# A trunk step on one core: reordering the normalization of the first token tile at the sub-layer boundaries

## The chip, the core and the metric

The kernel runs on one core of one Trainium2 chip. The metric is device time in microseconds (us) of one execution. Five engines run side by side, each through its own instruction list in order: TensorE (PE, matmuls), VectorE (DVE), ScalarE (ACT), GpSimd (POOL) and SyncE (SP, which starts the transfers here). They meet through semaphores only.

## What is computed

The reference is one step of a four-layer trunk over 128 context tokens and 256 sample tokens, model width 1024, all in fp32. Each layer has a half-step feed-forward (FFN), a mixer (attention, gated convolution or HGRN2) and a second FFN: twelve sub-layers. Cut to what matters here, every sub-layer is

```python
h = rmsnorm(x, g_pre) * (1 + scale) + shift        # modulated input of the sub-layer
o = sub_layer(h)                                   # ffn: (silu(h @ a) * (h @ b)) @ w_out
x = x + gate * rmsnorm(o, g_post)                  # and for an ffn half of it
```

So the input of each sub-layer needs the full output of the one before: two norms stand between the last product of one and the first product of the next.

## The kernel before, in words

**Tiles and products.** The 384 tokens are three tiles of 128 (t = 0, 1, 2). A product in full precision is made of three matmuls, high part times high part, high times low and low times high (`h_hi`, `h_lo` for the input, `w_hi`, `w_lo` for weights). Weights come in blocks of 128x1024; ACT rounds a block to its high part (line 1925), DVE subtracts for its low part (line 2081). The output of a sub-layer is summed in PSUM banks 0 to 5, bank 2t + n for tile t and column half n; an FFN's inner products use banks 6 and 7, a mixer's first ones banks 0 and 1.

**The end of a sub-layer.** `out_tail` (line 1757) does the last four row blocks of the output product tile by tile, so that tile 0 is ready first (lines 1720 to 1722, 24 matmuls per tile). The next input is then made tile by tile, in this chain, with e the number of the coming sub-layer (e = 1 to 11, so there are eleven such boundaries; seven lead into an FFN: e = 2, 3, 5, 6, 8, 9, 11, and four into a mixer: e = 1, 4, 7, 10):

- `out_squares` (ACT, line 1978) sums the squares of each half of the output in PSUM; `out_variance` (DVE, line 2172) and `out_root` (POOL, line 2358) make of it the factor of the post-norm; `gated` (DVE, line 2180) multiplies the output by the gate.
- `residual` (DVE, line 2193) adds it to `y`; `y_squares` (ACT, line 1990), `y_variance` (DVE, line 2172) and `y_root` (POOL, line 2363) make the factor of the pre-norm; `normed` (DVE, line 2208) writes `hn`.
- `turn_normed` (PE, line 1753) turns `hn` by 8 transposes into banks 2t and 2t + 1 (4 for the lower half of the width, k = 0 to 3, and 4 for the upper half, k = 4 to 7). So it can't run before `out_squares` and `gated` of that tile have read the bank.
- `modulate` (ACT, line 2002, 4 instructions for a half) reads the bank and writes `hf`; `hi_of` (DVE, line 2215) rounds it to `h_hi` for tiles 0 and 1; for tile 2 `hi_last` (DVE, line 2226) makes `h_hi` straight from PSUM, and its upper half waits for `modulate(e, 2, 1)`, since both read one bank.
- `lo_half` (POOL, line 2369) subtracts for `h_lo` of tiles 0 and 1, four instructions in the order upper half of both tiles, lower half of both; it starts when the upper half of tile 1 is rounded (`hi_of(e, 1, 1)`). `lo_last` (DVE, line 2236) does tile 2, two instructions.

**The start of the next sub-layer.** `first_tile` (PE, line 1710) multiplies tile 0 by the first two weight blocks, high input part alone: 8 row groups k, each of 4 matmuls. `first_blocks` (PE, line 1688) does the same for tiles 1 and 2, 32 matmuls that follow `hi_last` pair by pair, and then (line 1695) the low input part of all three tiles: 8 matmuls for the upper half, which wait for `lo_half` of the upper half and `lo_last(e, 1)`, and 8 for the lower half, which wait for all of `lo_half` and `lo_last(e, 0)`. Then the ordinary blocks run (lines 1671 to 1673).

**What sets the order.** It is written out by hand, one list in `boundary` for each engine: ACT's at line 2010, DVE's at line 2239, POOL's at line 2372 (unchanged), and PE's in `out_tail`. An engine that meets a wait holds all that stands behind it in its list. The first sub-layer (e = 0) and the end of the kernel have lists of their own. POOL's wait and the order of its work, as they stand:

```python
gp.wait_ge(h_high_made, 2 * (NT * e + NT - 2) + 2)
for half in (1, 0):
    for t in range(NT - 1):
        lo_half(e, t, half)
```

Of the kernel before, what the change touches and what calls it, by code (L numbers as in the profile page):

```python
# [16 lines left out]
DC = D // P  # L17
TP, TS = 128, 256
T = TP + TS
NT = T // P  # L20
# [73 lines left out]
def build(nc, ins, outs, n_sub=12):  # L94
# [1566 lines left out]
    def _(pe):  # L1661
# [35 lines left out]
                    if half == 0:  # L1697
                        last.then_inc(block_done, 1)

        def first_tile(s):  # L1700

            b0 = first_block[s]
            places = [(k, j) for k in range(DC) for j in range(2)]
            if s == 0:
                places = [(k, j) for j in range(2) for k in range(DC)]
            for k, j in places:
                pe.wait_ge(h_low_made if k < 4 else h_high_made, 2 * NT * s + 2)
                pe.wait_ge(w_lo_made, b0 + j + 1)
                for w in (w_hi, w_lo):
                    mm(psum[first_banks(s)[j]][:, 0:P], w[:, (b0 + j) % RING, k * P:(k + 1) * P], h_hi[:, k, 0:P],  # L1710
                       start=(k == 0 and w is w_hi), stop=False, skip_group_check=True)
# [33 lines left out]
            if t == NT - 1:  # L1745
                last.then_inc(block_done, 1)

        def turn_normed(e, t):

            for half in range(2):  # L1750
                pe.wait_ge(hn_made, 2 * (NT * e + t) + half + 1)
                for k in range(4 * half, 4 * half + 4):
                    last = nc.tensor.transpose(psum[2 * t + half][:, k % 4 * P:(k % 4 + 1) * P],  # L1753
                                               hn[:, t % 2, k * P:(k + 1) * P], ident)
                last.then_inc(hn_turned, 1)

        def out_tail(s, chunks, b):

            e = s + 1
            order = [(n, i) for n in range(2) for i in range(TAIL)]  # L1760
            late_last = [(n, i) for n in range(2) for i in range(TAIL - 1)] + [(0, TAIL - 1), (1, TAIL - 1)]
            for t in range(NT):
                for n, i in late_last if t == 0 else order:
                    if t == 0 and n == 0:
                        pe.wait_ge(w_lo_made, b + i + 1)
                        out_ready(s, chunks[i])
                    hi, lo = moving_out(s, chunks[i])
                    last = out_half(b + i, t, n, hi, lo, False, i == TAIL - 1)
                    if t == NT - 1 and n == 1:
                        last.then_inc(block_done, 1)  # L1770
                    elif i == TAIL - 1:
                        last.then_inc(acc_done, 1)
                    if t == NT - 1 and n == 0 and i == 0 and e < N_SUB:
                        turn_normed(e, 0)
            if e < N_SUB:
                turn_normed(e, 1)
                if sub_kind[s] == "ffn":
                    pe.wait_ge(a_read, FC * (ffn_number(s) + 1))
                    pe.wait_ge(b_read, FC * (ffn_number(s) + 1))
                    need(pe, mods_made, units_end[s])  # L1780

                pe.wait_ge(hf_low, NT * e + 1)
                pe.wait_ge(hf_high, NT * e + 1)
                first_tile(e)
                turn_normed(e, 2)

        def ada_half(half, bank, slab):

# [126 lines left out]
    def _(act):  # L1915
# [53 lines left out]
        def out_squares(e, t, n):  # L1969

            s = e - 1
            if t < NT - 1 or n == 0:
                act.wait_ge(acc_done, acc_number(s, t, n))
            else:
                act.wait_ge(block_done, first_block[e])
            number = square_number(e, t, n, False)
            act.wait_ge(squares_made, number - 2)
            A(junk[number % 3], psum[2 * t + n][:, :], ACT.Square, scale=1.0 / 32,  # L1978
              accum_out=o_ss[:, 2 * t + n:2 * t + n + 1]).then_inc(squares_made, 1)
# [13 lines left out]
        def modulate(e, t, half):  # L1993

            act.wait_ge(hn_turned, 2 * (NT * e + t) + half + 1)
            act.wait_ge(s_ready, e + 1)
            act.wait_ge(mods_made, 3 * e + 2)
            if t == NT - 1 and half == 0:
                act.wait_ge(h_low_made, 2 * NT * (e + 1))
            g = group_of(t)  # L2000
            for k in range(4 * half, 4 * half + 4):
                last = A(hf[:, t, k, :], psum[2 * t + half][:, k % 4 * P:(k % 4 + 1) * P], ACT.Identity,  # L2002
                         bias=mod[:, 3 * e * DC + k, g:g + 1], scale=s_cols[:, k, g:g + 1])
            last.then_inc(hf_high if half else hf_low, 1)
# [5 lines left out]
        def boundary(e):  # L2010
            if e > 0 and sub_kind[e - 1] in ("attn", "hgrn"):
                load_table(ACT.Silu)
            if e == N_SUB:
                for t in range(NT):
                    out_squares(e, t, 0)
                    out_squares(e, t, 1)
            elif e > 0:
                out_squares(e, 0, 0)
                out_squares(e, 0, 1)
                y_squares(e, 0)  # L2020
                out_squares(e, 1, 0)
                out_squares(e, 1, 1)
                modulate(e, 0, 0)
                y_squares(e, 1)
                out_squares(e, 2, 0)
                modulate(e, 0, 1)
                out_squares(e, 2, 1)
                modulate(e, 1, 0)
                y_squares(e, 2)
                modulate(e, 1, 1)  # L2030
                modulate(e, 2, 1)
                modulate(e, 2, 0)
            else:
                y_squares(e, 0)
                ada_copy(2, 6)
                y_squares(e, 1)
                y_squares(e, 2)
                ada_copy(0, 6)
                for t in range(NT - 1):
                    modulate(e, t, 0)  # L2040
                    modulate(e, t, 1)
                modulate(e, 2, 1)
                modulate(e, 2, 0)
            if e < N_SUB:
                for b in range(2, 6):
                    split(first_block[e] + b)
# [26 lines left out]
    def _(dve):  # L2073
# [101 lines left out]
        def gated(e, t, n):  # L2175

            s = e - 1
            dve.wait_ge(g_landed, 16 * e)
            dve.wait_ge(squares_made, square_number(e, t, n, False) + 1)
            V.tensor_tensor(og[:, t % 2, columns(n)], psum[2 * t + n][:, :], g_rows[:, group_of(t), columns(n)],  # L2180
                            ALU.mult).then_inc(og_made, 1)
# [57 lines left out]
        def boundary(e):  # L2239
            if e == 0:  # L2240
                for t in range(NT):
                    y_variance(e, t)
                for t in range(NT):
                    normed(e, t)
                for u in (1, 0):
                    ada_add(2 * u + 1, 6)
                    mod_add(u, 7)
                round_first(0)
                split(0)
                hi_of(e, 0, 0)  # L2250
                round_first(1)
                hi_of(e, 0, 1)
                split(1)
                hi_of(e, 1, 0)
                hi_last(e, 0)
                hi_of(e, 1, 1)
                hi_last(e, 1)
                lo_last(e, 1)
                lo_last(e, 0)
            elif e < N_SUB:  # L2260
                gated(e, 0, 0)
                out_variance(e, 0)
                gated(e, 0, 1)
                residual(e, 0)
                gated(e, 1, 0)
                y_variance(e, 0)
                normed(e, 0)
                out_variance(e, 1)
                gated(e, 1, 1)
                residual(e, 1)  # L2270
                hi_of(e, 0, 0)
                y_variance(e, 1)
                normed(e, 1)
                gated(e, 2, 0)
                hi_of(e, 0, 1)
                out_variance(e, 2)
                gated(e, 2, 1)
                residual(e, 2)
                hi_of(e, 1, 0)
                y_variance(e, 2)  # L2280
                normed(e, 2)
                hi_of(e, 1, 1)
                hi_last(e, 0)
                hi_last(e, 1)
                lo_last(e, 1)
                lo_last(e, 0)
            else:
                for t in range(NT):
                    gated(e, t, 0)
                    out_variance(e, t)  # L2290
                    gated(e, t, 1)
                    residual(e, t)
            if e < N_SUB:
                for b in range(2, 6):
                    split(first_block[e] + b)
# [158 lines left out]
```

## Time and profile before

| what | us |
|---|---|
| median of 3 runs | 3027.87 |
| lowest and highest of them | 3023.46, 3028.64 |
| span of the profiled execution (first to last instruction) | 3023.0 |
| what the median has beyond that span | 4.87 |
| TensorE busy in the span | 2968.9 (98%) |
| VectorE busy | 2194.7 (73%) |
| ScalarE busy | 1152.8 (38%) |
| GpSimd busy | 594.5 (20%) |

The profiled execution has no total of its own beside its span; the three times are of other executions of the same program. A matmul's record begins when it is issued, and its end is modelled: matmuls overlap, so the distance from one start to the next tells its cost, and "busy" counts more than that.

### The profile page before, as it was taken

To read this page: it belongs to the slowest core of one execution; us is meant where nothing else is said; L and a number is where in the kernel's file an instruction comes from. 1 tells how busy PE (TensorE), PEld (TensorE's weight loads), DVE (VectorE), ACT (ScalarE), POOL (GpSimd) and SP (SyncE) were. 2 spreads that over 40 slices of the span, in tenths; PEclk is the share of its full clock that TensorE was granted. 3 is DMA by queue.
4 is the path that set the end of the run, shared out by engine and by line. 5 is a ranking of instruction groups with operands and counts; after the bars stand their busy time and mean duration, and the time that the engine had idled before them with its cause. 6 is when DMAs were issued, how large, how long until landed. Compare 5 with 4: busy or idle time off the path is not lost.

```text
span 3023.0 us, 46915 instructions
## 1 busy us (share of the span) xinstructions
PE 2968.9 (98%) x18458; PEld 2750.8 (91%) x18458; DVE 2194.7 (73%) x2831; ACT 1152.8 (38%) x1966; POOL 594.5 (20%) x586
## 2 busy tenths in 40 slices
PE   7999999999999999999999999999999999999999
PEld 6999888999999998999899999979999999888998
DVE  6888678887877656888887576768887888775444
ACT  4222664223322424222422365553224222664222
POOL 1111212112211212112211144541122112211001
PEclk9999999999999999999999999999999999999999
DMA  8667435665665445766566443337675766333443
GB/s 303 208 212 215 138 86 190 209 209 168 212 210 172 117 134 166 222 211 197 181 209 202 133 117 95 103 96 230 209 215 166 222 211 197 110 79 119 126 127 96
DMA packets 565935, 515.61 MB, mean 171 GB/s; under 512 B 43013, under 2 KB 499286, under 8 KB 563926
## 3 DMA queue, kind: packets, MB, share of 16 engines
q1 hardware_dynamic: 565158, 512.37, 55.7%
q8 instruction: 148, 2.42, 0.3%
q14 instruction: 69, 0.57, 0.1%
q10 hardware_dynamic: 560, 0.25, 0.0%
HBM read 509.31 MB, written 3.24 MB: 170 GB/s over the span
## 4 chain that ended last, share of the span: by engine, by line
PE 91%; issue 3%; DVE 2%; ACT 1%; POOL 1%; DMA 1%; SPq 0%; DVEq 0%; POOLq 0%; ACTq 0%
PE bank L1671 19%; PE bank L1673 19%; PE bank L1672 19%; PE bank L1720 9%; PE bank L1722 9%; PE bank L1721 9%; PE bank L1688 2%; PE bank L1695 1%; PE bank L614 1%; PE bank L639 1%; PE bank L1753 1%; DMA ada_first<-w_ada 1%; POOL small L2358 0%; POOL small L2363 0%; ACT tmp L1978 0%
## 5 line engine op out<-in xcount | busy, mean ns | idle before, releaser
L1671 PE MATMUL bank<-h_hi,w_hi 128*128 128x384 f32 x3328 | 1120.7, 337 | 0.0
L1673 PE MATMUL bank<-h_hi,w_lo 128*128 128x384 f32 x3328 | 1115.1, 335 | 0.0
L1672 PE MATMUL bank<-h_lo,w_hi 128*128 128x384 f32 x3328 | 1114.0, 335 | 0.0
L1925 ACT ACTIVATE w_hi<-raw 128x1024 fp32r<-128x1024 f32 x646 | 680.5, 1061 | 1030.9 <-PE bank L1673 478.2
L2081 DVE TENSOR_TENSOR w_lo<-raw,w_hi 128x1024 fp32r<-128x1024 f32 x648 | 812.2, 1277 | 328.5 <-ACT w_hi L1925 323.6
L2108 DVE SCALAR_TENSOR_TENSOR fold<-ada_raw,cond,fold 128x1024 f32<-128x1024 f32 x462 | 638.7, 1439 | 0.1
L1671 PEld LDWEIGHTS bank<-h_hi,w_hi 128*128 128x128 f32 x3328 | 625.5, 188 | 10.9 <-ACT tmp L1944 1.6
L1672 PEld LDWEIGHTS bank<-h_lo,w_hi 128*128 128x128 f32 x3328 | 625.4, 188 | 6.1
L1673 PEld LDWEIGHTS bank<-h_hi,w_lo 128*128 128x128 f32 x3328 | 625.3, 188 | 0.0
L2399 POOL TENSOR_TENSOR h_lo<-tmp,h_hi 128x384 fp32r<-128x384 f32 x176 | 280.4, 1593 | 1737.6 <-DVE h_hi L2142 1737.6
L1720 PE MATMUL bank<-w_hi,h_hi 128*128 128x512 f32 x1056 | 415.4, 393 | 0.0
L1722 PE MATMUL bank<-w_hi,h_lo 128*128 128x512 f32 x1056 | 413.7, 392 | 0.0
L1721 PE MATMUL bank<-w_lo,h_hi 128*128 128x512 f32 x1056 | 413.2, 391 | 0.0
L1944 ACT ACTIVATE tmp<-bank 128x384 f32<-128x384 f32 x176 | 86.5, 491 | 481.4 <-PE bank L1673 479.1
L2138 DVE TENSOR_TENSOR tmp<-bank,tmp 128x384 f32<-128x384 f32 x176 | 97.9, 556 | 230.7 <-PE bank L1673 228.5
L1722 PEld LDWEIGHTS bank<-w_hi,h_lo 128*128 128x128 f32 x1056 | 198.2, 188 | 42.2
L1720 PEld LDWEIGHTS bank<-w_hi,h_hi 128*128 128x128 f32 x1056 | 198.3, 188 | 38.4
L1721 PEld LDWEIGHTS bank<-w_lo,h_hi 128*128 128x128 f32 x1056 | 198.3, 188 | 37.9
L2002 ACT ACTIVATE hf<-bank,mod,s_cols 128x128 f32<-128x128 f32 x288 | 106.5, 466 | 33.9 <-PE bank L1753 27.4
L2180 DVE TENSOR_TENSOR og<-bank,g_rows 128x512 f32<-128x512 f32 x72 | 49.3, 685 | 53.0 <-ACT tmp L1978 53.0
L1720 PE MATMUL bank<-w_hi,o_hi 128*128 128x512 f32 x192 | 77.1, 401 | 1.4 <-DVE tmp L942 1.0
L2115 DVE TRANSPOSE_TENSOR_REDUCE fold_sums<-fold 128x64 f32<-128x2048 f32 x33 | 76.0, 2304 | 0.0
(204 smaller groups left out, 2422.4 us busy)
## 6 DMA issues: line engine op xcount, KB each, us to landing
raw<-w_ffn_in SPq DMA_DIRECT2D x352, 512.0 KB, 5.0
ada_raw<-w_ada SPq DMA_DIRECT2D x264, 512.0 KB, 4.2
raw<-w_ffn_out SPq DMA_DIRECT2D x176, 512.0 KB, 4.6
raw<-w_hgrn_in SPq DMA_DIRECT2D x40, 512.0 KB, 4.0
g_rows<-g_dram SPq DMA_DIRECT2D x12, 1024.0 KB, 6.7
raw<-w_attn_qkv SPq DMA_DIRECT2D x24, 512.0 KB, 6.1
raw<-w_conv_in SPq DMA_DIRECT2D x24, 512.0 KB, 4.9
ada_first<-w_ada SPq DMA_DIRECT2D x16, 512.0 KB, 11.7
```

Of the source, the lines that this page charges most:

```text
L1671: mm(out, wh, h_hi[:, k, :], start=(k == 0), stop=False)
L1672: mm(out, wh, h_lo[:, k, :], start=False, stop=False)
L1673: last = mm(out, wl, h_hi[:, k, :], start=False, stop=(k == DC - 1))
L1720: mm(out, hi[:, tokens(t)], w_hi[:, b % RING, columns(n)], start=opens, stop=False)
L1721: mm(out, hi[:, tokens(t)], w_lo[:, b % RING, columns(n)], start=False, stop=False)
L1722: return mm(out, lo[:, tokens(t)], w_hi[:, b % RING, columns(n)], start=False, stop=closes)
L1925: A(w_hi[:, b % RING, :], raw[:, b % RAW, :], ACT.Copy).then_inc(w_hi_made, 1)
L2002: last = A(hf[:, t, k, :], psum[2 * t + half][:, k % 4 * P:(k % 4 + 1) * P], ACT.Identity, bias=mod[:, 3 * e * DC + k, g:g + 1], scale=s_c ...
L2081: V.tensor_tensor(w_lo[:, b % RING, :], raw[:, b % RAW, :], w_hi[:, b % RING, :].bitcast(F32), ALU.subtract).then_inc(w_lo_made, 1)
L2108: V.scalar_tensor_tensor(out=acc, in0=slab, scalar=c, in1=acc, op0=ALU.mult, op1=ALU.add).then_inc(fold_made, 1)
L2138: V.tensor_tensor(tmp[:, 2 + f % 2, :], psum[7][:, 0:T], tmp[:, f % 2, :], ALU.mult).then_inc(b_read, 1)
L2399: G.tensor_tensor(h2_lo[:, f % H2, :], tmp[:, 2 + f % 2, :], h2_hi[:, f % H2, :].bitcast(F32), ALU.subtract).then_inc(h2_lo_made, 1)
```

## The change

In all eleven boundaries ACT's and DVE's lists are reordered. ACT does `out_squares(e, 2, 1)` before `modulate(e, 0, 1)`, and `y_squares(e, 2)` before `modulate(e, 1, 0)`. DVE does `y_variance` and `normed` of tile 0 before `gated(e, 1, 0)`; `hi_of(e, 0, 1)` moves behind `residual(e, 2)`; `hi_of(e, 1, 0)` moves behind `normed(e, 2)`; and `hi_last(e, 0)` now stands ahead of `hi_of(e, 1, 1)`. POOL's list stays.

Where the coming sub-layer is an FFN (seven boundaries), PE's order changes too: only the lower half of tile 0 is turned inside the last tile's output product, its upper half behind it; row group 0 of `first_tile` comes before tile 1 is turned, groups 1, 2, 4, 5, 6, 3 after it, and group 7 after tile 2 is turned. The two waits for all of `modulate(e, 0, ...)` are dropped there, since banks 6 and 7 aren't the ones that it reads. In front of a mixer PE's order stays. No instruction is added or removed, and no transfer is touched.

```diff
--- before.py
+++ after.py
@@ -1697,10 +1697,10 @@
                     if half == 0:
                         last.then_inc(block_done, 1)
 
-        def first_tile(s):
+        def first_tile(s, ks=range(DC)):
 
             b0 = first_block[s]
-            places = [(k, j) for k in range(DC) for j in range(2)]
+            places = [(k, j) for k in ks for j in range(2)]
             if s == 0:
                 places = [(k, j) for j in range(2) for k in range(DC)]
             for k, j in places:
@@ -1745,9 +1745,9 @@
             if t == NT - 1:
                 last.then_inc(block_done, 1)
 
-        def turn_normed(e, t):
-
-            for half in range(2):
+        def turn_normed(e, t, parts=range(2)):
+
+            for half in parts:
                 pe.wait_ge(hn_made, 2 * (NT * e + t) + half + 1)
                 for k in range(4 * half, 4 * half + 4):
                     last = nc.tensor.transpose(psum[2 * t + half][:, k % 4 * P:(k % 4 + 1) * P],
@@ -1771,18 +1771,28 @@
                     elif i == TAIL - 1:
                         last.then_inc(acc_done, 1)
                     if t == NT - 1 and n == 0 and i == 0 and e < N_SUB:
-                        turn_normed(e, 0)
+                        turn_normed(e, 0, (0,) if sub_kind[e] == "ffn" else range(2))
             if e < N_SUB:
-                turn_normed(e, 1)
+                if sub_kind[e] == "ffn":
+                    turn_normed(e, 0, (1,))
+                else:
+                    turn_normed(e, 1)
                 if sub_kind[s] == "ffn":
                     pe.wait_ge(a_read, FC * (ffn_number(s) + 1))
                     pe.wait_ge(b_read, FC * (ffn_number(s) + 1))
                     need(pe, mods_made, units_end[s])
 
-                pe.wait_ge(hf_low, NT * e + 1)
-                pe.wait_ge(hf_high, NT * e + 1)
-                first_tile(e)
-                turn_normed(e, 2)
+                if sub_kind[e] == "ffn":
+                    first_tile(e, (0,))
+                    turn_normed(e, 1)
+                    first_tile(e, (1, 2, 4, 5, 6, 3))
+                    turn_normed(e, 2)
+                    first_tile(e, (7,))
+                else:
+                    pe.wait_ge(hf_low, NT * e + 1)
+                    pe.wait_ge(hf_high, NT * e + 1)
+                    first_tile(e)
+                    turn_normed(e, 2)
 
         def ada_half(half, bank, slab):
 
@@ -2023,10 +2033,10 @@
                 modulate(e, 0, 0)
                 y_squares(e, 1)
                 out_squares(e, 2, 0)
+                out_squares(e, 2, 1)
                 modulate(e, 0, 1)
-                out_squares(e, 2, 1)
+                y_squares(e, 2)
                 modulate(e, 1, 0)
-                y_squares(e, 2)
                 modulate(e, 1, 1)
                 modulate(e, 2, 1)
                 modulate(e, 2, 0)
@@ -2262,9 +2272,9 @@
                 out_variance(e, 0)
                 gated(e, 0, 1)
                 residual(e, 0)
-                gated(e, 1, 0)
                 y_variance(e, 0)
                 normed(e, 0)
+                gated(e, 1, 0)
                 out_variance(e, 1)
                 gated(e, 1, 1)
                 residual(e, 1)
@@ -2272,15 +2282,15 @@
                 y_variance(e, 1)
                 normed(e, 1)
                 gated(e, 2, 0)
-                hi_of(e, 0, 1)
                 out_variance(e, 2)
                 gated(e, 2, 1)
                 residual(e, 2)
-                hi_of(e, 1, 0)
+                hi_of(e, 0, 1)
                 y_variance(e, 2)
                 normed(e, 2)
+                hi_of(e, 1, 0)
+                hi_last(e, 0)
                 hi_of(e, 1, 1)
-                hi_last(e, 0)
                 hi_last(e, 1)
                 lo_last(e, 1)
                 lo_last(e, 0)
```

## Rows read from the trace of the kernel before

**Rows 1.** The page, busy time by engine over the whole span.
```profile
PE 2968.9 (98%) x18458; PEld 2750.8 (91%) x18458; DVE 2194.7 (73%) x2831; ACT 1152.8 (38%) x1966; POOL 594.5 (20%) x586
```

**Rows 2.** The view of waits, engine PE: total us, times, longest us.
```profile
PE bank L1753 <- DVE hn L2208: 16.3, 23, 1.3
```

**Rows 3.** Timeline of PE, boundary e = 3: start, us, instruction, count, idle before.
```profile
744.26 0.39 PE L1721 MATMUL bank<-w_lo,h_hi 128*128 128x512 f32 x1
744.49 0.39 PE L1722 MATMUL bank<-w_hi,h_lo 128*128 128x512 f32 x1
745.35 1.09 PE L1753 MATMUL bank<-base_k,hn 128*128 128x128 f32 x8 [0.47 <-DVE hn L2208]
...
751.10 1.03 PE L1753 MATMUL bank<-base_k,hn 128*128 128x128 f32 x8
751.89 0.30 PE L1710 MATMUL bank<-h_hi,w_hi 128*128 128x128 f32 x1
...
755.38 0.28 PE L1710 MATMUL bank<-h_hi,w_lo 128*128 128x128 f32 x1
756.59 1.09 PE L1753 MATMUL bank<-base_k,hn 128*128 128x128 f32 x8 [0.93 <-DVE hn L2208]
758.07 0.39 PE L1688 MATMUL bank<-h_hi,w_hi 128*128 128x256 f32 x1 [0.39 <-DVE h_hi L2226]
...
762.16 2.99 PE L1695 MATMUL bank<-h_lo,w_hi 128*128 128x384 f32 x16
765.03 0.44 PE L1671 MATMUL bank<-h_hi,w_hi 128*128 128x384 f32 x1
```

**Rows 4.** Timeline of DVE, the same boundary.
```profile
743.32 0.69 DVE L2180 TENSOR_TENSOR og<-bank,g_rows 128x512 f32<-128x512 f32 x1 [1.43 <-ACT tmp L1978]
...
744.81 0.88 DVE L2208 TENSOR_SCALAR hn<-y,small 128x512 f32<-128x512 f32 x2 [0.67 <-POOL small L2363]
...
752.96 1.42 DVE L2193 SCALAR_TENSOR_TENSOR y<-og,small,y 128x512 f32<-128x512 f32 x2
...
756.05 0.88 DVE L2208 TENSOR_SCALAR hn<-y,small 128x512 f32<-128x512 f32 x2 [0.66 <-POOL small L2363]
756.84 0.42 DVE L2215 CAST h_hi<-hf 128x512 fp32r<-128x512 f32 x1
757.28 1.37 DVE L2226 TENSOR_SCALAR h_hi<-bank,s_cols,mod 128x128 fp32r<-128x128 f32 x4
759.36 1.37 DVE L2226 TENSOR_SCALAR h_hi<-bank,s_cols,mod 128x128 fp32r<-128x128 f32 x4 [0.71 <-ACT hf L2002]
760.83 2.54 DVE L2236 TENSOR_TENSOR h_lo<-hf,h_hi 128x512 fp32r<-128x512 f32 x2
```

**Rows 5.** Timeline of ACT, the same boundary.
```profile
751.29 0.60 ACT L1978 ACTIVATE tmp<-bank 128x512 f32<-128x512 f32 x1 [0.56 <-PE bank L1722]
...
753.75 0.63 ACT L1990 ACTIVATE tmp<-y 128x512 f32<-128x512 f32 x1 [0.37 <-DVE y L2193]
...
757.72 2.90 ACT L2002 ACTIVATE hf<-bank,mod,s_cols 128x128 f32<-128x128 f32 x8 [1.20 <-PE bank L1753]
```

**Rows 6.** Timeline of POOL, the same boundary.
```profile
757.34 5.48 POOL L2369 TENSOR_TENSOR h_lo<-hf,h_hi 128x512 fp32r<-128x512 f32 x4 [1.33 <-DVE h_hi L2215]
```

**Rows 7.** The view of one line: count, ns of one (min/median/max), first and last start.
```profile
L2369 POOL TENSOR_TENSOR h_lo<-hf,h_hi x48: 1261/1293/2192, 37.0 to 2747.4; 128x512 fp32r<-128x512 f32 x48
```
```profile
L2236 DVE TENSOR_TENSOR h_lo<-hf,h_hi x24: 678/1252/1797, 42.4 to 2747.9; 128x512 fp32r<-128x512 f32 x24
```

**Rows 8.** Windows view, boundaries e = 8 and 9: busy (x), granted clock, DMA.
```profile
2030.90:2034.30 3.40, 3.40 (x16) 3.40 (x17) 2.59 (x8) 3.40 (x9) 3.40 (x4) 0.50 0.00 0
2314.20:2317.60 3.40, 3.32 (x14) 2.95 (x15) 2.12 (x7) 1.33 (x5) 2.56 (x3) 0.50 0.00 0
```

**Rows 9.** Timeline of PE, boundary e = 8: its first and last rows.
```profile
2018.08 1.09 PE L1753 MATMUL bank<-base_k,hn 128*128 128x128 f32 x8 [0.46 <-DVE hn L2208]
...
2039.05 0.44 PE L1671 MATMUL bank<-h_hi,w_hi 128*128 128x384 f32 x1
```

## The prediction

> **What bounds the kernel now.** The page comes first: PE is busy 98% of the span [rows 1], so only what makes PE stand still or issue less counts. The view of waits then says where PE stands still: its largest wait is for `hn` before the transposes of line 1753, 16.3 us, twice in nearly every boundary [rows 2]. The timelines of one boundary, e = 3, show what these waits are. The last product before tile 0's transposes starts at 744.49 and the next could at 744.72 (these start 0.23 us apart, 744.26 to 744.49), but the transposes start at 745.35: 0.63 us lost. Behind `first_tile` the last product starts at 755.38; the transposes of tile 2 could start at 755.49 and do at 756.59: 1.10 us lost. The transposes take 0.8 us (751.10 to 751.89), so tile 2's are issued by 757.4, and `first_blocks` starts at 758.07: some 0.6 us more [all rows 3]. That is 2.3 us a boundary, 26 us in eleven; no more than that can be won here.
>
> The reader should then look at POOL. Its four `lo_half` run 757.34 to 762.82 in one piece [rows 6], and the last 8 matmuls of line 1695 need all four. Line 1695 starts at 762.16 and the block behind it at 765.03 [rows 3]; half of its matmuls, 1.4 us, bring us to 763.55, when the lower half is wanted. So POOL is ready only 0.7 us before PE asks. A PE that is quicker by more than this, or a POOL that starts later, makes POOL the end of the boundary.
>
> **The change, part by part**, on the times of e = 3. Nothing is added, so each step is a shift; I lay each engine's new list out in order with the durations of the rows, an instruction starting when its engine is free and its inputs are there. The same laying out of the old lists gives 765.04 where the trace has 765.03.
>
> *Tile 0's norm.* `gated(e, 1, 0)` (743.32, 0.69 us) no longer stands ahead of it: `hn` starts at 743.55 in place of 744.81 [rows 4], PE finds it ready at 744.7 and wins the 0.63 us. What was moved behind it starts 1 us later, but `residual(e, 1)` still comes 0.65 us earlier, since POOL's roots now overlap DVE's work.
>
> *PE in front of an FFN.* Tile 2's product ends 1.1 us earlier, at 750.0 against 751.1, as also 4 of the 8 transposes moved out from inside it. Upper half of tile 0, row group 0 and tile 1 follow without a wait until 751.7, groups 1 and 2 until 752.6.
>
> *ACT.* `out_squares(e, 2, 1)` starts at 750.2 (751.29 before), `modulate(e, 0, 1)` behind it at 750.9 (749.2 before), to 752.4. `y_squares(e, 2)` starts at 752.7 (753.75 before [rows 5]), 1.1 us earlier. `modulate(e, 1, 0)` moves from 751.9 to 754.0, `modulate(e, 1, 1)` ends at 756.9, which nobody waits for yet.
>
> *DVE.* `residual(e, 2)` starts at 751.9 against 752.96 and `hn` of tile 2 at 755.0 against 756.05 [rows 4], 1.0 us earlier. But `hi_of(e, 0, 1)` stands behind that residual: it ends at 753.7, and row group 4 can't start before 753.8. **A new wait of 1.1 us** (752.6 to 753.8) takes the place of the old one; the tail that queues behind it is tile 2's transposes, which start at 755.6, 1.0 us earlier than before. `first_blocks` follows at 757.0 (758.07 before) and line 1695 at 761.2 (762.16 before): PE is 0.95 us ahead.
>
> *What is late next: POOL.* It starts behind `hi_of(e, 1, 1)`. Before, that stood right behind `normed(e, 2)` and ended at 757.26. Now `hi_of(e, 1, 0)` (0.42) and `hi_last(e, 0)` are ahead of it; `hi_last(e, 0)` needs tile 2's transposes (756.2) and takes 1.28 us, so `hi_of(e, 1, 1)` ends at 757.96 and POOL starts at 758.04, 0.7 us **later**. And its time grows. Before, three of the four took about 1.27 us and the last 1.75, beside `lo_last(e, 0)`; `lo_last` itself takes 0.68 us or up to 1.80 [rows 7], and its two here last 2.54 us [rows 4]. I read this as one of the two engines held while the other reads: DVE's `lo_last(e, 1)` came in between POOL's third and fourth, and POOL lost 0.45 us. Now `lo_last(e, 1)` is asked for at 759.9, while POOL is at its second, and `lo_last(e, 0)` at 761.0, while it is at its third: two holds, 0.9 us. POOL ends at 758.04 + 4 x 1.27 + 0.9 = 764.0 (762.82 before), and the lower half of line 1695 starts at 764.1 in place of 763.55. **Each FFN boundary is 0.5 us longer, 7 x 0.5 = 3.6 us.** Bounds for this term: no hold at all ends POOL at 763.1 (-0.4 us each), two full durations of 0.68 end it at 764.5 (+1.0). I take 0.45 for a hold, the measured one of this same pair.
>
> The Trainium skill, "SBUF — State Buffer", section "SBUF: two separate sides", says that VectorE with two SBUF inputs and GpSimd exclude each other for the whole instruction, and that the first to start wins. By its rule the sum has both holds, +0.5 us; had the trace's 1.75 been a lone accident, the sum would be near -0.1 a boundary. The trace agrees with the rule as far as it goes (1.75 against 1.27 us).
>
> *In front of a mixer.* PE's order stays, so `first_tile` waits for `modulate(e, 0, 1)`, and this is now behind `out_squares(e, 2, 1)`, which waits for the end of tile 2's product. PE would be there at 751.2 (all eight transposes are inside) and starts at 752.9: 1.0 us later than before. Tile 2's transposes start at 756.5 (756.59 before), so PE comes out even. `hi_of(e, 1, 1)`, behind `hi_last(e, 0)`, ends at 758.9, 1.6 us later than before; with the second hold POOL ends at 764.9 and the lower half starts at 765.0 against 763.55. **Each mixer boundary is 1.5 us longer, 4 x 1.5 = 5.9 us.** With no hold it is 0.6, with full ones 1.9.
>
> *Hidden at nothing.* The splits of the next weight blocks stand behind `lo_last(e, 0)` on DVE. The first now ends at 765.1, and the block that needs it starts at 765.6: 0.4 us of cover left; were it gone, each further tenth would be paid eleven times. No transfer, and nothing on SP's queue, moves.
>
> *The clock.* In four boundaries (e = 1, 5, 8, 9) the granted clock fell to 0.50, 1.2 GHz, for 3.4 us [rows 8], two of the four shown and the others alike, each time behind the short products and waits around tile 2's transposes. Its price: e = 8 takes 20.97 us from tile 0's transposes to the next block [rows 9], e = 3 takes 765.03 - 745.35 = 19.68 [rows 3], so 1.29 us, some 4.8 us for the four. If POOL ends the boundary, PE has 1.4 us to spare ahead of it, and a fall during `first_blocks` costs nothing; only one that hits tile 2's transposes still costs 0.4 to 0.7. I take 3.5 us back; the bounds are 4.8 and, see the first rival, a loss.
>
> **Sum:** 3.6 + 5.9 - 3.5 = +6.0 us on the span of 3023.0. The profiled execution has no time beside its span; I add the 4.87 us between span and median, so 3027.9 + 6.0 = 3034 us.
>
> **The rivals.** (1) *The clock falls more often.* For: PE now stands still for 1.1 or 1.5 us inside the short products and again 1.4 us ahead of the last 8 matmuls. Against: the second wait lies between dense matmuls, and no fall in rows 8 lies there. If half of the boundaries lose 1.7 us (half of 3.4) where nothing hides it, the 3.5 us aren't won and 9 are lost or less: up to +18, likely 3042. (2) *The holds don't repeat.* With one hold the FFN boundaries cost 0.1 and the mixers 1.0, +4.7 less 3.5; with none 0 less 3.5: 3024 to 3029, likeliest 3028. (3) *The other side: POOL doesn't end the boundary.* Then PE's gain of 0.95 us stands at the seven FFN boundaries, the mixers are even, and the clock's 3.5 us come on top: -10, 3018. It decides at POOL's end: it would have to be ready by 762.6, with a start at 758.04 and never less than 1.26 us an instruction [rows 7], which is 763.1 at the best. That speaks strongly against it. (4) *The change does nothing that lasts:* the delay is taken up behind the boundary. PE's 98% speaks against it: 3028.
>
> **How the numbers follow.** My forecast has a chance of 0.60, spread some 4 us around 3034; rival 1 has 0.15, rival 2 0.17, rival 3 0.05, rival 4 0.03. A measurement of this kernel tells about 0.2%, 6.06 us, from no change. So the forecast's own 0.60 falls about 0.33 slower and 0.27 the same; with rival 1 slower is 0.48, with 2 and 4 the same is 0.47, and faster is rival 3. The forecast's own range is 3030 to 3038; to hold 8 in 10 it goes down to rival 2 with its clock gain and up to rival 1: 3025 to 3042.
>
> **What would show it.** Right: in FFN boundaries no wait before line 1753, one of 1.1 us inside line 1710, and one of about 1.4 us in the middle of line 1695's 16 matmuls; `lo_half` as a group of 6 us that starts behind `hi_last(e, 0)`, with two of its four near 1.7 us; in mixer boundaries a wait of about 1.5 us before line 1710; fewer falls of the clock, or falls that cost nothing. Wrong: line 1695 running as one piece, or POOL's group ending before PE asks. Then the sum's largest terms are gone, and the time is that of rival 3.

## The result and the profile after

| | kernel before | changed kernel |
|---|---|---|
| median (lowest to highest), us | 3026.79 (3023.46 to 3028.64), 4 runs | 3042.69 (3040.51 to 3045.39), 4 runs |
| profiled execution, span | 3023.0 | 3038.7 |
| mean granted clock of TensorE | 0.997 | 0.992 |

The change makes the kernel slower: the ratio of the times is 1.0053 (95% interval 1.0041 to 1.0065), some 16 us. Forecast were +6 us and a range up to 3042. The direction was right, the size was not. The profiled execution of the changed kernel took 3040.51 us with a span of 3038.7, so 1.8 us lie around a span, and not the 4.87 that I added.

Where does PE stand still now? The view of waits of the changed kernel, engine PE (total us, times, longest):

```profile
...
PE bank L1695 <- POOL h_lo L2379: 7.7, 9, 1.1
PE bank L1710 <- ACT hf L2012: 6.6, 4, 1.7
PE bank L1710 <- DVE h_hi L2225: 6.5, 7, 0.9
...
PE bank L1753 <- DVE hn L2218: 0.9, 1, 0.9
```

Above these rows the view has one wait of 9.6 us for a transfer at the start of the kernel, which the kernel before has too. The first three rows take the place of [rows 2]: the waits for `hn`, 23 with 16.3 us, are down to one with 0.9, and what replaces them is POOL's low parts, nine times, ACT's `modulate` ahead of `first_tile`, four times (the mixers), and DVE's rounding inside `first_tile`, seven times (the FFNs). (The changed kernel has ten more lines ahead of ACT's list, so ACT's 2002 is 2012, DVE's 2208, 2215, 2226 and 2236 are 2218, 2225, 2236 and 2246, POOL's 2369 is 2379. PE's lines are the same.)

The timeline of PE in the changed kernel, the same boundary e = 3 as in [rows 3]:

```profile
745.84 0.60 PE L1753 MATMUL bank<-base_k,hn 128*128 128x128 f32 x4
...
751.07 0.60 PE L1753 MATMUL bank<-base_k,hn 128*128 128x128 f32 x4
751.43 0.30 PE L1710 MATMUL bank<-h_hi,w_hi 128*128 128x128 f32 x1
...
751.91 1.06 PE L1753 MATMUL bank<-base_k,hn 128*128 128x128 f32 x8
...
754.74 0.33 PE L1710 MATMUL bank<-h_hi,w_hi 128*128 128x128 f32 x1 [0.93 <-DVE h_hi L2225]
...
756.58 1.08 PE L1753 MATMUL bank<-base_k,hn 128*128 128x128 f32 x8
...
758.05 0.39 PE L1688 MATMUL bank<-h_hi,w_hi 128*128 128x256 f32 x1
...
762.28 1.66 PE L1695 MATMUL bank<-h_lo,w_hi 128*128 128x384 f32 x8
765.01 1.69 PE L1695 MATMUL bank<-h_lo,w_hi 128*128 128x384 f32 x8 [1.07 <-POOL h_lo L2379]
766.58 0.44 PE L1671 MATMUL bank<-h_hi,w_hi 128*128 128x384 f32 x1
```

This boundary starts 1.12 us later in its profile than that of [rows 3] in its own (739.23 against 738.11, by the ruler below), so 1.12 us are to be taken off before the two are compared: line 1688 starts at 756.93 against 758.07, the block of line 1671 at 765.46 against 765.03. The transposes wait for nothing. Line 1695, one group of 16 in [rows 3], has split into 8 and 8, with 1.07 us of standing still between them. POOL and DVE of the same boundary, against [rows 6] and [rows 4]:

```profile
759.04 5.92 POOL L2379 TENSOR_TENSOR h_lo<-hf,h_hi 128x512 fp32r<-128x512 f32 x4 [3.05 <-DVE h_hi L2225]
```

```profile
756.82 0.42 DVE L2225 CAST h_hi<-hf 128x512 fp32r<-128x512 f32 x1
757.26 1.36 DVE L2236 TENSOR_SCALAR h_hi<-bank,s_cols,mod 128x128 fp32r<-128x128 f32 x4
758.55 0.42 DVE L2225 CAST h_hi<-hf 128x512 fp32r<-128x512 f32 x1
759.44 1.37 DVE L2236 TENSOR_SCALAR h_hi<-bank,s_cols,mod 128x128 fp32r<-128x128 f32 x4 [0.47 <-ACT hf L2012]
760.91 2.93 DVE L2246 TENSOR_TENSOR h_lo<-hf,h_hi 128x512 fp32r<-128x512 f32 x2
```

POOL starts behind the second `CAST`, which stands behind four `TENSOR_SCALAR` of `hi_last`, and its four last 5.92 us in place of 5.48.

**A ruler for all eleven.** To compare kernels I measure each boundary in their timelines from the start of ACT's first `out_squares` to the start of the first matmul behind line 1695. It is the same work in every kernel:

| boundary (the sub-layer that comes) | before | changed |
|---|---|---|
| e = 1, mixer | 28.15 * | 28.55 |
| 2, FFN | 26.91 | 27.34 |
| 3, FFN | 26.92 | 27.35 |
| 4, mixer | 27.23 | 31.24 * |
| 5, FFN | 27.80 * | 27.66 * |
| 6, FFN | 26.89 | 28.27 * |
| 7, mixer | 26.86 | 31.38 * |
| 8, FFN | 28.18 * | 27.33 |
| 9, FFN | 28.20 * | 27.54 * |
| 10, mixer | 26.85 | 30.31 * |
| 11, FFN | 26.91 | 27.34 |
| sum | 300.9 | 314.3 |

The star marks boundaries in which the granted clock fell to 0.50 (1.2 GHz). The sum grew by 13.4 of the span's 15.7 us. The other 2.3 lie outside the boundaries: 1.9 in the HGRN sub-layer, where the changed kernel's profile has two falls and the one of before has one, 1.1 in the first attention, and -0.8 ahead of the first boundary.

Without a fall an FFN boundary grew from 26.91 to 27.34, by 0.43 us (forecast 0.5), a mixer boundary from 26.86 to 28.55, by 1.7 us (forecast 1.5). The falls are the surprise. The windows view of the changed kernel (width, busy time and count of PE, PEld, DVE, ACT, POOL, granted clock, DMA), for e = 1 without a fall and for e = 4, 7, 10:

```profile
318.00:324.00 6.00, 5.38 (x46) 5.17 (x47) 4.05 (x12) 5.24 (x16) 0.55 (x1) 1.00 0.00 0
1037.00:1048.90 11.90, 11.32 (x56) 10.98 (x57) 6.38 (x17) 7.84 (x22) 3.10 (x4) 0.57 0.01 2
1752.00:1762.30 10.30, 10.30 (x49) 9.93 (x49) 4.65 (x15) 6.48 (x19) 2.77 (x3) 0.50 0.01 2
2608.70:2615.60 6.90, 6.90 (x33) 6.53 (x33) 3.21 (x9) 4.13 (x13) 1.29 (x2) 0.51 0.01 2
```

[rows 8] had falls of 3.4 us; two of these last 10.2 us, one 6.8. The timeline of PE in e = 4 tells what was at work:

```profile
1037.58 0.30 PE L1710 MATMUL bank<-h_hi,w_hi 128*128 128x128 f32 x1 [1.64 <-ACT hf L2012]
1037.71 0.28 PE L1710 MATMUL bank<-h_hi,w_lo 128*128 128x128 f32 x1
...
1042.82 0.41 PE L1710 MATMUL bank<-h_hi,w_lo 128*128 128x128 f32 x1
1043.03 0.41 PE L1710 MATMUL bank<-h_hi,w_hi 128*128 128x128 f32 x1
...
1043.46 1.93 PE L1753 MATMUL bank<-base_k,hn 128*128 128x128 f32 x8
```

`first_tile` starts 0.11 us apart, behind the wait for `modulate`, and is 0.21 us apart at its end; the transposes take 1.93 us in place of 1.06. All of this lies ahead of `hi_last(e, 0)`, and so ahead of POOL's start. POOL and the low input part in e = 4:

```profile
1046.35 5.93 POOL L2379 TENSOR_TENSOR h_lo<-hf,h_hi 128x512 fp32r<-128x512 f32 x4 [6.54 <-DVE h_hi L2225]
```

```profile
1050.84 3.18 PE L1695 MATMUL bank<-h_lo,w_hi 128*128 128x384 f32 x16
```

POOL ends at 1052.28, and the ninth of these 16 matmuls starts at 1052.34, 0.28 us behind the eighth in place of 0.17. So POOL still ends the boundary, by 0.1 us; in e = 7 it is 0.3 us. That is why the view of waits has POOL nine times and not eleven: in these two the fall had slowed PE so much that the two came nearly together.

### The profile page after: what moved, and what is told of

It reads as the page before. It is cut to its first block, busy times and chain, and to the rows that moved or that the text cites. A ratio compares the mean times of both kernels' runs of the same rounds, so it can differ in the third digit from the quotient of the medians.

```text
span 3038.7 us, 46908 instructions
## 1 busy us (share of the span) xinstructions
PE 2983.6 (98%) x18458; PEld 2765.1 (91%) x18458; DVE 2208.7 (73%) x2831; ACT 1152.9 (38%) x1966; POOL 603.5 (20%) x586
## 4 chain that ended last, share of the span: by engine, by line
PE 91%; POOL 2%; issue 2%; DVE 2%; ACT 1%; DMA 1%; SPq 0%; another core or an unknown queue 0%; DVEq 0%; POOLq 0%; ACTq 0%
PE bank L1671 19%; PE bank L1673 19%; PE bank L1672 19%; PE bank L1720 10%; PE bank L1722 9%; PE bank L1721 9%; POOL h_lo L2379 2%; PE bank L614 1%; PE bank L1695 1%; PE bank L639 1%; PE bank L1710 1%; DMA ada_first<-w_ada 1%; DVE h_hi L2236 0%; PE bank L1753 0%; PE bank L1057 0%
## 5 line engine op out<-in xcount | busy, mean ns | idle before, releaser
L2091 DVE TENSOR_TENSOR w_lo<-raw,w_hi 128x1024 fp32r<-128x1024 f32 x648 | 823.8, 1295 | 328.4 <-ACT w_hi L1935 323.6
L2379 POOL TENSOR_TENSOR h_lo<-hf,h_hi 128x512 fp32r<-128x512 f32 x48 | 71.7, 1524 | 58.6 <-DVE h_hi L2225 58.6
```

Source lines behind the costliest of these rows:

```text
L2091: V.tensor_tensor(w_lo[:, b % RING, :], raw[:, b % RAW, :], w_hi[:, b % RING, :].bitcast(F32), ALU.subtract).then_inc(w_lo_made, 1)
L2379: G.tensor_tensor(h_lo[:, ks, tokens(t)], hf[:, t, ks, :], h_hi[:, ks, tokens(t)].bitcast(F32), ALU.subtract).then_inc(h_lo_made, 1)
```

## The experiments

Theory after the result, in two parts. (S) Schedule: POOL's low parts end last, because `hi_of(e, 1, 1)` stands behind `hi_last(e, 0)` and DVE holds POOL up twice. (C) Clock: PE's new wait ahead of `first_tile` in front of a mixer draws the clock down, for longer than before and where nothing hides it. The rival to C: falls are chance, spread over all boundaries. Each kernel was measured beside the kernel before on the same chip. The kernel before had medians of 3025.80 to 3027.06 us there, so a difference from the changed kernel's 3042.69, measured apart from them, is sure to a microsecond or two only. Each kernel has one profiled execution, and where the clock falls in it is one sample.

**1. Old lists in front of the mixers.**

ACT's list, where the two differ; DVE's is split in the same way.

```diff
+if sub_kind[e] == "ffn":
     out_squares(e, 2, 1)
     modulate(e, 0, 1)
     y_squares(e, 2)
     modulate(e, 1, 0)
+else:
+    modulate(e, 0, 1)
+    out_squares(e, 2, 1)
+    modulate(e, 1, 0)
+    y_squares(e, 2)
```

> The changed kernel, but in front of the four mixers ACT's and DVE's lists are those of before. Theory (the clock is drawn down by PE's wait ahead of first_tile in front of a mixer, and costs there 8 us or so; the rest is POOL's late low parts): the mixer boundaries are back at 26.9 us each, with no fall of 10 us; the FFN boundaries stay at 27.3 where the clock doesn't fall. Total 3 to 6 us above before. Rival (how often the clock falls is chance, spread over all boundaries): the mixers' schedule gives back 6.6 us, and the long falls are met at the FFN boundaries as well; total 8 us or more above before.

Measured: 3028.88 us (3026.99 to 3034.18), ratio 1.0010 (1.0001 to 1.0019). The mixer boundaries take 26.86, 27.20, 26.89 and 26.87 us, none with a fall. The FFN boundaries take 27.34 to 27.37 without a fall; two of the seven have one of 3.4 us. The kernel is 2.8 us above before, so what was done in front of the four mixers made some 13 of the 16 us.

**2. Old lists in front of the FFNs**, PE's order there too.

ACT's list; DVE's is split in the same way.

```diff
+if sub_kind[e] == "ffn":
+    modulate(e, 0, 1)
+    out_squares(e, 2, 1)
+    modulate(e, 1, 0)
+    y_squares(e, 2)
+else:
     out_squares(e, 2, 1)
     modulate(e, 0, 1)
     y_squares(e, 2)
     modulate(e, 1, 0)
```

> The changed kernel, but in front of the seven FFNs all three lists are those of before. Theory: three of the four mixer boundaries or so still have falls of 7 to 10 us, each boundary 28.6 us without a fall and 30 to 31.4 with one, and the FFN boundaries are 26.9; total 11 to 14 us above before. Rival (chance): the mixers' falls are rare now, total 7 us above.

Measured: 3037.58 us, ratio 1.0035 (1.0022 to 1.0049), 11.5 us above before. Mixer boundaries: 30.80, 31.06, 28.42 and 29.84 us, so three of four have a fall again, of 6.8, 10.2 and 6.8 us; e = 7 has none. FFN boundaries without a fall: 26.90 to 26.93, but for e = 9 with 27.24; e = 8 has one of 3.4 us. With 1, this speaks against chance: among the boundaries of these two kernels the long falls go with the mixers' lists.

**3. The wait filled.** Does PE's standing still bring the falls? The lists stay, PE is only kept at work. (The fillers read the first weight block, so a wait for that block comes with them; PE doesn't stand still at it in the profile.)

```diff
 # PE, out_tail, in front of a mixer
+b0 = first_block[e]
+pe.wait_ge(w_lo_made, b0 + 1)
+for _ in range(8):
+    mm(psum[6][:, :], w_hi[:, b0 % RING, 0:P], w_hi[:, b0 % RING, 0:512], start=True, stop=True)
 pe.wait_ge(hf_low, NT * e + 1)
```

> The changed kernel with 8 matmuls of 512 columns that nobody reads, put into PE's wait ahead of first_tile in front of a mixer (1.8 us of work in a wait of 1.95). Theory: no schedule changes, but the clock doesn't fall there any more: mixer boundaries all at 28.6 us, total some 7 us below the changed kernel. Rival (the falls come from elsewhere in the boundary, or the fall's cost was hidden anyway): the same time as the changed kernel within 2 us, or slower by the fillers if they delay first_tile.

Measured: 3031.97 us (3029.25 to 3034.66), ratio 1.0019 (1.0010 to 1.0029), about 11 us below the changed kernel's 3042.69. Eight more matmuls in each of four places made the kernel faster. Mixer boundaries: 28.44, 28.43, 28.41 and 28.43 us. The windows view of this kernel, over the four of them:

```profile
316.00:328.00 12.00, 11.61 (x89) 10.78 (x88) 8.95 (x20) 11.13 (x29) 4.74 (x5) 1.00 0.00 0
1035.00:1047.00 12.00, 11.61 (x90) 10.76 (x88) 9.04 (x21) 10.75 (x28) 4.25 (x5) 1.00 0.01 3
1749.00:1761.00 12.00, 10.54 (x79) 9.72 (x79) 9.68 (x17) 9.95 (x22) 7.44 (x6) 1.00 0.01 3
2603.00:2615.00 12.00, 10.51 (x72) 9.69 (x72) 10.80 (x16) 10.46 (x20) 8.20 (x6) 1.00 0.04 11
```

The granted clock is 1.00 in all. The wait on POOL in the middle of line 1695 is still there (1.09 us in e = 4), so C and S are separate: this took C away in front of the mixers and left S. It won 4 us more than I expected. Between the two profiles the spans differ by 7.8 us, 7.5 of them in the boundaries, although four FFN boundaries have a fall here (three in the changed kernel). The rest of the 11 us lies in executions without a profile: the profiled one of the changed kernel was the fastest of its four, the one here is above its median.

**4. POOL earlier.** The same for S: one wait changed, nothing else.

```diff
 # POOL, boundary(e)
-gp.wait_ge(h_high_made, 2 * (NT * e + NT - 2) + 2)
+gp.wait_ge(h_low_made, 2 * (NT * e + NT - 2) + 2)
```

> The changed kernel with one wait of POOL changed: its low parts start behind hi_of(e,1,0) and no longer behind hi_of(e,1,1), the order of the four is kept. Theory (POOL's end sets the boundary where the clock stays up): the lower half of line 1695 starts 1.1 us earlier, boundaries without a fall go from 27.3 to 26.2 us (FFN) and from 28.6 to 27.4 (mixer), total 8 to 12 us below the changed kernel. Rival (POOL isn't what PE waits for, or DVE's rounding is held up by POOL as much as is won): 0 to 3 us below.

Measured: 3030.34 us (3025.34 to 3031.94), ratio 1.0012 (1.0003 to 1.0022), 12 us below the changed kernel. FFN boundaries without a fall take 26.26 to 26.29 us, 1.1 less; e = 8 and 9 have one and take 26.96 and 26.98. POOL in e = 3:

```profile
757.77 1.28 POOL L2379 TENSOR_TENSOR h_lo<-hf,h_hi 128x512 fp32r<-128x512 f32 x1 [1.33 <-DVE h_hi L2225]
759.49 4.25 POOL L2379 TENSOR_TENSOR h_lo<-hf,h_hi 128x512 fp32r<-128x512 f32 x3 [0.44 <-DVE h_hi L2225]
```

One of the four is done before the others may start. The mixers still have falls (of 6.8 us, 29.4 to 29.8 us in all four). So the changed lists and PE's new order in front of the FFNs did together win time, 0.6 us against the 26.9 of before, and POOL took it all back and 0.4 more.

**5. The upper half first.** The same cause from DVE's side, at a price for PE.

```diff
 # DVE, boundary(e)
 hi_of(e, 1, 0)
+hi_of(e, 1, 1)
 hi_last(e, 0)
-hi_of(e, 1, 1)
 hi_last(e, 1)
```

> The changed kernel with hi_of(e,1,1) back ahead of hi_last(e,0) on DVE. POOL starts 0.6 us (FFN) and 1.1 us (mixer) earlier, but hi_last(e,0) and with it first_blocks come 1.0 and 0.5 us later. Theory (POOL's end is what counts): without falls FFN boundaries go from 27.3 to 26.9 and mixers from 28.6 to 27.5 us, though first_blocks starts later; total 7 us below the changed kernel, the mixers' falls as they are. Rival (first_blocks' start is what counts): slower than the changed kernel by 5 us or more.

Measured: 3029.39 us (3026.94 to 3034.61), ratio 1.0010 (1.0001 to 1.0019). Without a fall FFN boundaries take 26.96 to 27.01 us and mixers 27.4. The mixers e = 7 and 10 have falls of 10.2 us and take 31.0; four FFN boundaries have falls too, e = 5, 6 and 11 of 3.4 us (27.07, 27.90 and 27.09 us) and e = 8 of 6.8 us (28.70), so a long fall isn't bound to the mixers. The expected 7 us were 13; the FFNs' 0.4 and the mixers' 1.2 make 7.6, and what is more came without a part of it that I can point to. PE's timeline in e = 3:

```profile
760.10 0.38 PE L1688 MATMUL bank<-h_hi,w_hi 128*128 128x256 f32 x1 [1.06 <-DVE h_hi L2236]
...
764.03 3.26 PE L1695 MATMUL bank<-h_lo,w_hi 128*128 128x384 f32 x16
```

PE waits 1.06 us before `first_blocks`, which it didn't in the changed kernel, and the boundary is still shorter, since line 1695 is in one piece: what counted was POOL's end, not PE's start.

**6. ACT's pair back** in front of the mixers, DVE's list as changed.

```diff
 # ACT, boundary(e), in front of a mixer
-out_squares(e, 2, 1)
 modulate(e, 0, 1)
+out_squares(e, 2, 1)
```

> The changed kernel, but in front of a mixer ACT does modulate(e,0,1) ahead of out_squares(e,2,1) again; DVE's list stays the changed one. PE's wait ahead of first_tile goes, and one of 1.1 us comes up inside it, for hi_of(e,0,1) behind residual(e,2). Theory: without falls a mixer boundary takes 0.5 us less than 28.55, and the falls there are fewer or shorter than with a wait of 1.95 us: total 5 to 9 us below the changed kernel. Rival (any wait of over 1 us at that place draws the clock down as much): boundaries of 30 us remain, total 2 us below the changed kernel.

Measured: 3031.61 us (3027.05 to 3036.12), ratio 1.0014 (1.0005 to 1.0024), 11 us below the changed kernel. It is more than the 5 to 9 us that I expected. Mixer boundaries: 27.75, 28.35, 28.01 and 29.28 us, of which 4, 7 and 10 have falls, of 3.4, 3.4 and 6.8 us; without a fall that is 0.8 us less than 28.55. So a wait of 0.9 us inside `first_tile` still brings falls, but shorter ones than the wait of 1.7 us ahead of it, and cheaper: 0.3 to 1.5 us against 1.8 to 2.8.

**7. The moved norm alone,** on the kernel before. Is the change's first piece worth what it should be?

```diff
 # DVE, boundary(e), of the kernel before
 residual(e, 0)
-gated(e, 1, 0)
 y_variance(e, 0)
 normed(e, 0)
+gated(e, 1, 0)
```

> The kernel before with the change's first piece alone: DVE does y_variance and normed of tile 0 ahead of gated(e,1,0). Theory (this piece wins PE's 0.63 us wait before the first transposes and pulls all that follows along, and the loss of the whole change comes from the other pieces): each boundary 0.64 us shorter, 26.3 in place of 26.9 us, total 7 us below before, the falls of the clock as before. Rival (the wait moves on to the next step, tile 2's transposes or POOL): boundaries within 0.2 us of 26.9, total within 2 us of before.

Measured: 3018.63 us (3014.95 to 3022.87), ratio 0.9973 (0.9963 to 0.9983): 8.4 us below the kernel before, and so faster than both kernels. Boundaries without a fall take 26.19 to 26.23 us, 0.7 less, mixers and FFNs alike (e = 9: 26.57); six of the eleven have one, which costs 0.9 to 1.3 us. PE in the boundary e = 3:

```profile
741.79 1.04 PE L1753 MATMUL bank<-base_k,hn 128*128 128x128 f32 x8
747.47 1.03 PE L1753 MATMUL bank<-base_k,hn 128*128 128x128 f32 x8
752.96 1.09 PE L1753 MATMUL bank<-base_k,hn 128*128 128x128 f32 x8 [0.93 <-DVE hn L2208]
```

The 0.47 us ahead of tile 0's transposes are gone and the 0.93 ahead of tile 2's are as they were: the whole chain behind the first wait moved up with it.

**8. The same, with PE kept busy.**

```diff
 # PE, out_tail
 first_tile(e)
+for _ in range(4):
+    mm(psum[0 if sub_kind[e] == "ffn" else 6][:, :], w_hi[:, first_block[e] % RING, 0:P],
+       w_hi[:, first_block[e] % RING, 0:512], start=True, stop=True)
 turn_normed(e, 2)
```

> The one before this, with 4 matmuls of 512 columns that nobody reads put between first_tile and tile 2's transposes in all eleven boundaries (0.9 us of work in a wait of 1.1). Theory (falls of the clock come from PE standing still there): no boundary has a fall, all take 26.3 us; total 9 to 12 us below before. Rival (fillers don't keep the clock up, or they delay the transposes): as norm_alone, or up to 0.2 us a boundary above it.

Measured: 3015.04 us (3012.74 to 3019.78), ratio 0.9965 (0.9952 to 0.9977), the fastest kernel here. No boundary has a fall; ten take 26.14 to 26.23 us, e = 9 takes 26.55. Its profiled execution isn't better than that of 7 (spans 3018.0 and 3018.4), since its falls elsewhere were longer: 13.7 us of half clock at the start of the kernel, 3.4 there in 7, and three in the HGRN sub-layer. Against 7 the gain is some 3.6 us between medians; the two intervals overlap.

**9. The clock alone,** the fillers of 8 on the kernel before, its lists untouched.

> The kernel before, its lists untouched, with the 4 unread matmuls between first_tile and tile 2's transposes in all eleven boundaries. It prices the clock by itself. Theory: all eleven boundaries take 26.9 us and none has a fall; total 3 to 6 us below before (its profile showed four falls, 1.2 us each). Rival (fillers cost what they save): within 1 us of before.

Measured (expected were 3 to 6 us below before): 3023.31 us against 3025.80 for before, measured beside it, ratio 0.9992 (0.9983 to 1.0001). No boundary has a fall; they take 26.86 to 26.95 us but for e = 4 (27.25) and e = 9 (27.28), and their sum is 296.7 against 300.9. So the falls cost the kernel before 4.2 us in the profile that the forecast rests on (the 27.2 of e = 4 and the 27.3 of e = 9 come without a fall; I didn't look for their cause). Between medians it is 2.5 us, which the interval doesn't tell from nothing.

**10. Combined:** the changed lists with POOL early (experiment 4) in front of the FFNs, experiments 7 and 8 in front of the mixers.

> In front of the seven FFNs the changed kernel's lists with POOL starting behind hi_of(e,1,0); in front of the four mixers the lists of before with y_variance and normed of tile 0 moved ahead, and the 4 unread matmuls before tile 2's transposes. It asks whether the rest of the change has worth of its own once POOL isn't late. Theory (PE's new order wins no more than the moved norm alone): FFN boundaries 26.3 us without a fall and up to 0.7 more with one, mixers 26.2; total within 3 us of the moved norm with fillers. Rival (the new order pays once POOL is early): FFN boundaries below 26.0, total 3 us or more below it.

Measured: 3017.68 us (3015.04 to 3018.62), ratio 0.9971 (0.9960 to 0.9981). FFN boundaries without a fall 26.27, and four with one at 26.96 to 27.22; mixers 26.16 to 26.19. The lists in front of the FFNs hold the moved norm too. With POOL mended all of them and PE's new order together are worth what the one moved norm is worth alone (26.2), and no more. The kernel is 2.6 us above that of experiment 8, whose fillers it lacks in front of the FFNs.

## Why the prediction was right and where it was wrong

- **Tile 0's norm, 0.63 us: right.** The wait before the first transposes is gone, and alone it is worth 0.7 us a boundary, 8.4 us in all (experiment 7).
- **The new wait inside `first_tile`, 1.1 us: right.** Seven times, 0.93 of it shown as standing still; PE starts `first_blocks` about 1 us sooner, as said.
- **POOL late, and held twice: right.** In e = 3 PE stood still for 1.07 us in the middle of line 1695; the four took 5.92 us (4 x 1.27 + 0.9 = 6.0 forecast). In the mean over the kernel they went from 1.40 to 1.52 us each. That it is POOL's end that counts is shown twice, by experiments 4 and 5. In the changed kernel's e = 3 POOL's third and fourth last 1.75 and 1.71 us, its first two 1.29. That the 0.45 us of a hold are the exclusion of two engines fits these durations; no run changed that alone. The Trainium skill, "SBUF — State Buffer", section "SBUF: two separate sides", says that a VectorE instruction with two SBUF inputs and a GpSimd instruction that reads SBUF exclude each other for the whole instruction, and the two holds agree with it.
- **The two terms of the schedule: right.** 7 x 0.5 + 4 x 1.5 = 9.5 us were forecast; 7 x 0.43 + 4 x 1.7 = 9.8 are what boundaries without a fall show (e = 4 of before already took 0.37 more, so 9.4 by the table).
- **The clock: wrong, and of the wrong sign.** The step that failed is "I take 3.5 us back". The table gives 8.7 us for the falls of the changed kernel (314.3 less 7 x 27.34 and 4 x 28.55) against 4.7 before (300.9 less 296.2): 4.0 lost, not 3.5 won, a difference of 7.5 us (experiment 9 puts the falls of before at 4.2). It rested on the prediction's "if POOL ends the boundary, PE has 1.4 us to spare", which is so in kind, with 1.1 us to spare by the trace, for a fall that begins with tile 2's transposes or later (e = 5 and e = 9: 27.66 and 27.54, only 0.2 to 0.3 us; in e = 6 it began 0.8 us sooner and cost 0.9). But the wait ahead of the mixers' `first_tile` put the falls further up, over `first_tile` and tile 2's transposes, where POOL's start hangs on them, and they lasted up to 10.2 us, not the 3.4 of rows 8. Rival 1 had this mechanism, with a chance of 0.15. That its 3042 meets the measured 3042.69 is in part luck: it reckoned with an even 1.7 us in half of the boundaries, and the table has 0.2 to 2.8 us in six of them. Against it I had argued that the second wait lies between dense matmuls; the experiments say so too, but it was the first wait that did it.
- **What is left** of the 16 us, 2.3 us in the two profiles, lies outside the boundaries; the sum had no term for it. With it the account of the spans closes: 15.7 measured less 6.0 forecast is 9.7 us, of which 7.5 are the clock's, 2.3 this, and -0.1 the schedule's. In the twelve kernels' profiles the stretch with the HGRN sub-layer takes 254.1 to 258.6 us, with one to three falls, whatever the lists are. Whether the change has any part in that is open; no run was made for it.

## What to carry to other kernels

Before moving work forward on the engine that bounds the kernel, lay out the lists of all engines in a stage by hand. That gave the schedule's part here to 0.2 us a boundary, and showed that the helper with 0.7 us of slack, idle 80% of the time, would end last. Cut a change of an order into its pieces: one moved line won 8 us, and the rest lost 24. And treat a wait of the matmul engine in a stretch of short matmuls as having a second price, through its clock, that can be larger than the wait: where the wait can't go, matmuls that nobody reads can be faster than none.

## What the runs showed of the hardware that I had not expected

The granted clock can stay at 0.50 for 10.2 us although PE is at work all the time (10.30 us busy of 10.30, with 49 matmuls, in e = 7). Ahead of it stands a wait of 1.6 us, then come 32 matmuls of 128 columns, and at 1.2 GHz these are stretched from 0.11 to 0.21 us apart. Whether that is why it stays down was not tried.

Experiment 3 shows that PE's standing still is what starts it: with 8 matmuls of 512 columns in place of the wait, four of four boundaries kept 1.00. A wait of 1.6 to 1.7 us there doesn't always bring a fall. It did in three of four mixer boundaries of the changed kernel, in three of four in experiment 2, in four of four in experiment 4 and in two of four in experiment 5, which makes 12 of 16.
